# Prompt attention scores over the 64 rows of their own head, without the zero-padded queries

## The reference, cut to what matters

```python
FOX_HEADS = 16
FOX_DH = D_MODEL // FOX_HEADS          # 64
FOX_SCALE = FOX_DH ** -0.5
Q_BLOCK = 128
    def one_block(args):
        qi, ci, pi = args
        s = jnp.einsum('bqhd,bkhd->bhqk', qi, k).astype(jnp.float32) * FOX_SCALE
        s = s + jnp.swapaxes(ci, 1, 2)[..., :, None] - cum_k[:, :, None, :]
        mask = (kpos[None, :] <= pi[:, None]) & valid[None, :]
        p = jax.nn.softmax(jnp.where(mask, s, MASK_VALUE), axis=-1)
        return jnp.einsum('bhqk,bkhd->bqhd', p.astype(v.dtype), v)
```

## Time and profile before

| what | us |
|---|---|
| median of three runs | 2298.31 (2297.2 to 2301.33) |
| span of the profiled execution | 2295.4 |
| what lies around the span (median less span) | 2.9 |
| prompt attention, first bias to first page of the sample attention | 1396.1 to 1572.5 |
| PE busy | 2099.1 (91%) |
| DVE, ACT, POOL busy | 887.8, 621.2, 581.0 |

### The profile page before, as it was taken

The page is one execution under the profiler, slowest core; times in us unless marked ns, Lnnn a source line. Parts: engine busy times, 40 slices in busy tenths (PEclk is TensorE's granted clock), DMA queues, the critical chain, the costliest instruction groups (busy, mean ns, idle before and its releaser), DMA issues.

```text
span 2295.4 us, 37322 instructions
## 1 busy us (share of the span) xinstructions
PE 2099.1 (91%) x16087; PEld 1932.8 (84%) x16087; DVE 887.8 (39%) x989; ACT 621.2 (27%) x725; POOL 581.0 (25%) x132
## 2 busy tenths in 40 slices
PE   5989999999979999999796997988787889999998
PEld 5969879888869999999796995665555789999998
DVE  4344352453465142435442234552222354334241
ACT  4222322322242111112322134443333131111121
POOL 2303404214033333333232231000000123333331
PEclk8999999999989999999998998999999899999999
DMA  4341342332422222221324110005887312222221
GB/s 145 111 156 38 111 165 65 129 120 92 147 83 74 74 89 75 73 91 56 100 73 140 57 55 10 1 1 207 326 326 299 102 56 77 89 73 88 77 73 59
DMA packets 168640, 240.01 MB, mean 105 GB/s; under 512 B 12898, under 2 KB 131810, under 8 KB 168210
## 3 DMA queue, kind: packets, MB, share of 16 engines
q1 hardware_dynamic: 156738, 214.11, 27.7%
q10 hardware_dynamic: 11712, 23.76, 2.8%
q0 software_dynamic: 80, 0.52, 0.1%
HBM read 212.26 MB, written 26.12 MB: 104 GB/s over the span
## 4 chain that ended last, share of the span: by engine, by line
issue 51%; PE 31%; POOL 9%; ACT 3%; DVE 2%; DMA 2%; SPq 1%; POOLq 0%; ACTq 0%
POOL w_lo L660 9%; PE PS L705 7%; PE PS L704 7%; PE PS L706 7%; PE PS L1028 2%; DMA k_page<-in_cache_k 2%; PE PS L1003 1%; PE PS L1064 1%; PE PS L1026 1%; PE PS L1082 1%; ACT k_page_t L1453 1%; PE PS L1075 1%; PE PS L1114 1%; PE PS L1011 1%; ACT probs_t L1432 1%
## 5 line engine op out<-in xcount | busy, mean ns | idle before, releaser
L660 POOL TENSOR_TENSOR w_lo<-w_raw,w_hi 128x2048 fp32r<-128x2048 f32 x125 | 578.0, 4624 | 1671.9 <-ACT w_hi L1188 1671.9
L704 PE MATMUL PS<-x_hi,w_hi 128*128 128x296 f32 x1792 | 540.5, 302 | 24.0 <-DVE x_lo L1526 18.2
L1188 ACT ACTIVATE w_hi<-w_raw 128x2048 fp32r<-128x2048 f32 x125 | 239.6, 1917 | 1129.3 <-PE PS L706 893.9
L705 PE MATMUL PS<-x_lo,w_hi 128*128 128x296 f32 x1792 | 541.0, 302 | 0.0
L706 PE MATMUL PS<-x_hi,w_lo 128*128 128x296 f32 x1792 | 538.7, 301 | 0.0
L704 PEld LDWEIGHTS PS<-x_hi,w_hi 128*128 128x128 f32 x1792 | 341.7, 191 | 27.7 <-issue 23.2
L705 PEld LDWEIGHTS PS<-x_lo,w_hi 128*128 128x128 f32 x1792 | 341.4, 190 | 0.3 <-issue 0.2
L706 PEld LDWEIGHTS PS<-x_hi,w_lo 128*128 128x128 f32 x1792 | 341.1, 190 | 0.0
L705 PE MATMUL PS<-hidden_lo,w_hi 128*128 128x296 f32 x1024 | 307.2, 300 | 0.0
L706 PE MATMUL PS<-hidden_hi,w_lo 128*128 128x296 f32 x1024 | 306.1, 299 | 0.0
L704 PE MATMUL PS<-hidden_hi,w_hi 128*128 128x296 f32 x1024 | 305.8, 299 | 0.0
(11 more groups left out here) (205 smaller groups left out, 2470.8 us busy)
## 6 DMA issues: line engine op xcount, KB each, us to landing
w_raw<-in_w_mlp_up SPq DMA_DIRECT2D x32, 1024.0 KB, 5.3
w_raw<-in_w_mlp_down SPq DMA_DIRECT2D x32, 1024.0 KB, 5.0
k_page<-in_cache_k SPq DMA_DIRECT2D x64, 512.0 KB, 6.1
v_page<-in_cache_v SPq DMA_DIRECT2D x64, 512.0 KB, 6.5
w_raw<-in_w_ret_in SPq DMA_DIRECT2D x24, 1024.0 KB, 5.3
sample_state<-in_state_ret SPq DMA_DIRECT2D x32, 512.0 KB, 5.4
out_state_ret_sample<-sample_state ACTq DMA_DIRECT2D x32, 512.0 KB, 4.3
w_raw<-in_w_ret_out SPq DMA_DIRECT2D x16, 512.0 KB, 3.4
```

Of the source, the lines that this page charges most:

```text
L660: pool.tensor_tensor(WL[n.slot][:], WR[n.slot][:], WH[n.slot][:].bitcast(F32), ALU.subtract) \
L704: pe.matmul(o, wh[:, w], xh[:, t, cols], start=(t == 0), stop=False)
L705: pe.matmul(o, wh[:, w], xl[:, t, cols], start=False, stop=False)
L1188: act.activation(WH[n.slot][:], WR[n.slot][:], ACT.Copy).then_inc(hi_done, 1)
```

## The change

`scores` reads the queries of a head from `QT` itself, 64 rows, and the keys from the same 64 rows of `KTT`. `QZ`, its two zeroings on POOL, its 16 copies on DVE and the two semaphores go. The products of bias, their shapes and the order on PE stay.

```diff
-        QZ = [place(f"q_by_head{i}", [P, 2, NPROMPT], TOK0 + 8 * NPROMPT * i)[0] for i in range(2)]
...
-        qz_zero = sem("qz_zero")
-        qz_done = sem("qz_done")
...
-            pool.wait_ge(lfc_ready, 1)
-            for i in range(2):
-                pool.memset(QZ[i][:], 0.0).then_inc(qz_zero, 1)
...
                 pieces = [(a, min(a + 512, n)) for a in range(0, n, 512)]
-                if j % 4 == 0:
-                    pe.wait_ge(qz_done, t + 1)
                 for a, e in pieces:
                     pe.matmul(score_cols(j, par)[:, a:e], NSR[:, P * (2 * t + par):P * (2 * t + par) + P], CU[:, a:e],
                               start=True, stop=False)
                 for a, e in pieces:
-                    last = pe.matmul(score_cols(j, par)[:, a:e], QZ[t % 2][:, par, P * (j % 4):P * (j % 4) + P],
-                                     KTT[:, t, NSAMP + a:NSAMP + e], start=False, stop=True)
+                    own = slice(DH * par, DH * par + DH)
+                    q = W0 + P * (j % 4)
+                    last = pe.matmul(score_cols(j, par)[:, a:e], QT[own, t, q:q + P], KTT[own, t, NSAMP + a:NSAMP + e],
+                                     start=False, stop=True)
...
-            def by_pair(t):
-                for par in range(2):
-                    h = slice(DH * par, DH * par + DH)
-                    ins = dve.tensor_copy(QZ[t % 2][h, par, :], QT[h, t, W0:T])
-                ins.then_inc(qz_done, 1)
-
-            dve.wait_ge(qz_zero, 2)
-            dve.wait_ge(tok_evac, 2 * KT)
-            by_pair(0)
             maximum(0, 0)
...
-                if j % 4 == 0 and j + 4 < 4 * KT:
-                    by_pair(j // 4 + 1)
```

## The result

The forecast was 2306.1 us, with a range of 2299 to 2314. Measured were 2348.61 us as the median of four runs (2333.89, 2336.53, 2360.69, 2361.59), against 2299.82 for the kernel before beside them (four runs, 2297.2 to 2302.48). The ratio is 1.0213, with a 95% interval of 1.0157 to 1.0268. The change costs about 49 us, six times what was forecast, and the time lies far above the range. The runs also differ by 28 us among themselves, where those of before differ by 5.

What follows compares the result with a forecast made beforehand. PE was taken to bound the stage. New tile steps, 7.3 us in the blocks, and +0.5 at the start, with 0.8 gained there counted, summed to +7.8 on 2298.31, giving 2306.1 us; range 2299 to 2314.

Steps and rivals of the forecast that it cites:

- What bounds the stage, what goes: Changed stage: PE sets the pace; POOL's zeroings and 14 of DVE's 16 copies are hidden, so removing them gains nothing.
- the first pair's 0.8 us: Stage start: the first two query copies delay PE's first bias; removing them gains 0.8 us, once.
- Streaming unchanged: Score products: 64 rows stream the same 144 to 528 key columns, so the products themselves cost no change.
- The price of a step: PE going between 128-row bias and 64-row scores: 0.15 us a step, 0.19 at half clock, 98 new steps.
- Rival 1, no price: Steps between 128 and 64 rows cost nothing, 2297.5 us, or half of them cost, about 2301; chance 0.17 together.
- Rival 2, two heads at once: Scores of a plane's two heads, in different array rows, overlap on PE: 2292 us; chance 0.03.
- Rival 3, all steps exposed: Waits for ACT move along with PE and hide no steps: +14 us, 2312; chance 0.07.
- the likeliest case: The forecast, steps between 0.07 and 0.17 us: ACT waits fall from 1.4 to near 0.8 a plane; chance 0.68.
- Rival 4, the clock falls: Steps idle PE more, each plane has 3 us at half clock, 1.5 lost: 12 us more, 2318; chance 0.05.

Runs made afterwards that it cites:

- run with 128 steps: Kernel before plus one 16-column product over 64 rows between bias and scores of every head: 2326.82 us, ratio 1.0121.
- run with 61 steps and 64 rows: Changed kernel with bias and scores of both heads over rows 0 to 63, so they share a tile: 2330.1 us, ratio 1.0177.

## Why the prediction was wrong, point by point

- **What bounds the stage, what goes.** Right. PE sets the pace; without the copies and with 128-row products the time is the same within 0.1% (the run with full rows), and the first pair's 0.8 us is in the trace.
- **Streaming unchanged.** Not contradicted at full clock: two records over 64 rows and a step out take 0.87 us, and the step accounts for what is above the 0.67 of two records.
- **The price of a step.** The size was nearly right: 0.19 in block 0, where 0.15 was forecast, and a plane of 22.09 us, forecast 22.0. The source of the price, the change between 16 and 128 rows in the values, was a good neighbour. The Trainium skill, "TensorEngine Tiling (Array Packing)", under Key Properties, says that changing the tiling mode drains the engine; the 0.57 us of "issue" behind the 400-key scores agree with it.
- **Rival 1, no price.** Wrong. The main evidence for it, the turning without idle time, was of a tile narrower in columns. A change of rows cost at both start rows.
- **Rival 2, two heads at once.** Rightly refused for this order, and its mechanism is real: with the biases moved, two heads take the time of one.
- **Rival 3, all steps exposed.** Wrong; the wait for ACT fell from 1.4 to 0.8 a plane, as the likeliest case had it.
- **Rival 4, the clock falls.** This is where the prediction failed. Its sum costs all products and steps behind the start at a granted clock of 1.00 and has no term for a fall; as a rival the fall was given a chance of 0.05 and 12 us. The runs show 29 of the stage's 40 us in that missing term. The argument against it was that "PE stays at 1.00 with its 2.1 us of idle time a plane now, and no single wait grows". That judged the clock by PE's idle time alone, as the kernel before has it. The run with 128 steps shows the idle moments of the steps to be harmless (0.99 from 1405 to 1570), and the run with 61 steps and 64 rows has the fall (0.81). Waits that the kernel before bears at 1.00 stand ahead of falls once products over 64 rows are beside them. Nothing in the trace of before alternates with products over 64 rows through a whole stage, so no row bore on it; the honest course was to call that term unknown and to let it stretch the range. Its size was also too small: the 3 us at half clock a plane, 24 in all, came from no row, and the trace shows 73 more than before. The loss in each was taken as 0.50, and it was 0.40.

In the sum of 40 us for the stage, steps are about 8, the clock about 29. The forecast of +7.8 was a good forecast of the first and lacked the second.

What is not settled: why the first head's product costs clock and the second's doesn't; why the clock returns to 1.00 at 1428.6 and 1513.9 and falls again between; and why the clock is lower behind the stage in the run with small steps. The runs show that with scores over 128 rows the granted clock holds 1.00 through the body of the stage, and that with scores over 64 their order, PE's waits and filler in these waits decide how long it is down. What the chip measures to decide it, they don't show.

## What to carry to other kernels

Zeros that pad a contraction to the full 128 rows need not be waste if the copies that make them lie beside other work: here they kept PE's clock at its upper level and its tiles alike. Before a dense stretch of PE is narrowed in rows, look at its neighbours' tiles (a step was 0.15 to 0.19 us at full clock, once in and once out) and treat the granted clock as an unknown that the trace of before cannot answer; it was worth 40% here of every microsecond at the lower level. If 64-row products are wanted, put those of different row halves side by side, where two took the time of one, but only where PE gets no longer wait by it: that order cost 0.2% in two blocks of four and 2.0% in three. Read the granted clock of the stage first in the result.

## What was unexpected of the hardware

- The granted clock stayed at 1.2 GHz for 16 us in which PE was busy without a gap in the records. The kernel before, with longer waits, had 2.4 GHz in the same stage.
- Useless products over 128 rows in PE's waits took a kernel from 2348.61 and 2352.05 us to 2320.38.
- The loss is not proportional: the second head alone over 64 rows cost 0.12%, the first alone 0.74%, both 2.1 to 2.6%.
- Two 64-row products of 400 columns each, in different halves of the rows, took 0.87 us together, as did one alone, each time with a step behind.
- The kernel whose clock goes up and down in the stage has runs far apart: 28 and 29 us between the lowest and the highest, in order of their mean clock.
